# Rotary halves exchanged by lane shuffles on VectorE, with signed sine tables, where a constant matrix product did it

## What is computed

```python
def apply_rope(x, ang):
    cos = jnp.cos(ang)[None, :, None, :].astype(x.dtype)
    sin = jnp.sin(ang)[None, :, None, :].astype(x.dtype)
    x1, x2 = jnp.split(x, 2, axis=-1)
    return jnp.concatenate([x1 * cos - x2 * sin, x1 * sin + x2 * cos], axis=-1)

# in first_block:
qa_rope = apply_rope(qa_rope, ang_1d)                       # 8 heads, the last 32 of 96 features
k_pe = apply_rope(k_pe[:, :, None, :], ang_1d)              # one key, shared by the 8 heads
qb = jnp.concatenate([apply_rope(qr, ang_row), apply_rope(qc, ang_col)], axis=-1)   # 8 heads of 64
kb = jnp.concatenate([apply_rope(kr, ang_row), apply_rope(kc, ang_col)], axis=-1)   # 2 heads of 64
...
merged = jax.nn.sigmoid(gate_a) * ya + jax.nn.sigmoid(gate_b) * yb
```

## Time and profile before

| | us |
|---|---|
| median of three runs | 2274.43 |
| lowest, highest run | 2272.1, 2279.98 |
| span of the profiled execution | 2278.4 |
| TensorE busy in it | 2195.7 |
| VectorE busy in it | 1152.1 |
| ScalarE busy in it | 817.9 |
| GpSimd busy in it | 25.3 |

### The profile page before, as it was taken

How to read it: one execution, slowest core, us unless ns; L and a number is a source line. 1 busy time by engine, 2 the same in 40 slices (tenths; PEclk the granted TensorE clock), 3 DMA queues, 4 the chain that set the end, 5 groups by cost and what they waited for, 6 DMA issues and landing times. The chain is left out here.

```text
span 2278.4 us, 26492 instructions
## 1 busy us (share of the span) xinstructions
PE 2195.7 (96%) x10904; PEld 1735.5 (76%) x10904; DVE 1152.1 (51%) x1705; ACT 817.9 (36%) x1169; POOL 25.3 (1%) x22
## 2 busy tenths in 40 slices
PE   8999999999999998999988999999899998999998
PEld 6776668888888886887976888887686576888886
DVE  5456666542442577678745444422733636444423
ACT  4313663331232364442433322212514734332212
POOL 0001000000000000000000000000000000000000
PEclk9999999999999998999899999999999999999999
DMA  4221012322222222234112222222232021222221
GB/s 175 76 74 38 1 38 77 108 92 103 93 93 93 92 66 87 93 121 101 48 56 74 93 93 93 93 93 93 80 119 98 2 93 56 96 90 96 99 99 66
DMA packets 43113, 190.77 MB, mean 84 GB/s; under 512 B 15520, under 2 KB 16224, under 8 KB 22384
## 3 DMA queue, kind: packets, MB, share of 16 engines
q1 hardware_dynamic: 40656, 184.84, 24.1%
q10 hardware_dynamic: 2336, 4.23, 0.6%
HBM read 185.32 MB, written 3.74 MB: 83 GB/s over the span
## 5 line engine op out<-in xcount | busy, mean ns | idle before, releaser
L240 DVE TENSOR_TENSOR weights_low<-weights_raw,weights_high 128x2048 fp32r<-128x2048 f32 (+1 forms) x164 | 372.6, 2272 | 574.5 <-ACT weights_high L213 574.5
L421 PE MATMUL psum<-split,weights_high 128*128 128x512 f32 (+1 forms) x1496 | 598.2, 400 | 13.6 <-DVE weights_low L240 5.6
L423 PE MATMUL psum<-split,weights_low 128*128 128x512 f32 (+1 forms) x1496 | 597.0, 399 | 0.0
L422 PE MATMUL psum<-split,weights_high 128*128 128x512 f32 (+1 forms) x1496 | 592.7, 396 | 0.0
L213 ACT CAST weights_high<-weights_raw 128x2048 fp32r<-128x2048 f32 (+1 forms) x164 | 309.7, 1888 | 577.3 <-PE psum L423 545.1
L421 PEld LDWEIGHTS psum<-split,weights_high 128*128 128x128 f32 (+1 forms) x1496 | 282.3, 189 | 83.6 <-issue 11.6
L422 PEld LDWEIGHTS psum<-split,weights_high 128*128 128x128 f32 (+1 forms) x1496 | 282.5, 189 | 71.5 <-issue 1.7
L423 PEld LDWEIGHTS psum<-split,weights_low 128*128 128x128 f32 (+1 forms) x1496 | 282.3, 189 | 67.1
L423 PE MATMUL psum<-hidden_high,weights_low 128*128 128x512 f32 x256 | 102.1, 399 | 0.0
L422 PE MATMUL psum<-hidden_low,weights_high 128*128 128x512 f32 x256 | 100.9, 394 | 0.0
L421 PE MATMUL psum<-hidden_high,weights_high 128*128 128x512 f32 x256 | 100.4, 392 | 0.0
(11 more groups left out here) (463 smaller groups left out, 3069.4 us busy)
## 6 DMA issues: line engine op xcount, KB each, us to landing
weights_raw<-in_weights SPq DMA_DIRECT2D x161, 1024.0 KB, 4.8
minus_c<-minus_c_rows ACTq DMA_DIRECT2D x16, 256.0 KB, 8.4
x_stream<-in_x SPq DMA_DIRECT2D x4, 512.0 KB, 7.1
gdn_in_grown<-gdn_rows SPq DMA_DIRECT2D x4, 512.0 KB, 4.7
chain_grown<-gdn_rows SPq DMA_DIRECT2D x4, 512.0 KB, 4.0
out<-end_results SPq DMA_DIRECT2D x8, 256.0 KB, 2.0
table<-rope_tables SPq DMA_DIRECT2D x1, 1024.0 KB, 12.5
weights_raw<-in_weights SPq DMA_DIRECT2D x1, 768.0 KB, 4.3
```

The source lines that it names most:

```text
L240: self.nc.vector.tensor_tensor(out=self.low[:, n % 2, 0:width], in0=self.raw[:, n % 2, 0:width], in1=self.high[:, n % 2, 0:width].bitcast( ...
L421: nc.tensor.matmul(bank, wh, ah, start=first, stop=False)
L422: nc.tensor.matmul(bank, wh, al, start=False, stop=False)
L423: return nc.tensor.matmul(bank, wl, ah, start=False, stop=last)
```

## The change

The constant matrix `rotate` is dropped, and with it `rotate_tile` and its waits on TensorE. On VectorE each rotation first shuffles the partitions of its tile within each group of 32 (`stream_shuffle` with the list `other_half`, lane l takes lane l + 16 modulo 32) from the tile into `turned`. The minus sign that the matrix carried moves into the sine tables, which are negative for the first half of each group. The order then is: wait until the tile is normed (for `qk_b`), shuffle, wait for it, tile times cosine in place, `turned` times sine in place, wait for both, sum. All inputs of the two products now lie in SBUF. The loop's assignment of rotations to gates stays.

```diff
--- before.py
+++ after.py
@@ -50,7 +50,7 @@
 
 CONST_AT = {}
 _col = 0
-for _name, _n in [("identity", P), ("rotate", P), ("heads_of_pair", 2), ("ones", 1), ("causal_bias", P),
+for _name, _n in [("identity", P), ("heads_of_pair", 2), ("ones", 1), ("causal_bias", P),
                   ("earlier", P), ("before", P), ("not_after", P), ("eye", SOLVE * SOLVE)]:
     CONST_AT[_name] = (_col, _n)
     _col += _n
@@ -69,9 +69,6 @@
     row, col = np.arange(P)[:, None], np.arange(P)[None, :]
     put("identity", row == col)
 
-    half = ROPE // 2
-    first = (col % ROPE) < half
-    put("rotate", np.where(first & (row == col + half), -1.0, 0.0) + np.where(~first & (row == col - half), 1.0, 0.0))
     put("heads_of_pair", (row // HD_B) == np.arange(2)[None, :])
     put("ones", 1.0)
 
@@ -94,13 +91,13 @@
     for half in range(2):
         at = NOPE + half * (ROPE // 2)
         out[0, at:at + ROPE // 2] = np.cos(ang)
-        out[1, at:at + ROPE // 2] = np.sin(ang)
+        out[1, at:at + ROPE // 2] = np.sin(ang) if half else -np.sin(ang)
     row_ang = ((t // GRID_W).astype(np.float32)[None, :] * inv[:, None]).astype(np.float32)
     col_ang = ((t % GRID_W).astype(np.float32)[None, :] * inv[:, None]).astype(np.float32)
     for group in range(P // 16):
         a = row_ang if (group // 2) % 2 == 0 else col_ang
         out[2, group * 16:(group + 1) * 16] = np.cos(a)
-        out[3, group * 16:(group + 1) * 16] = np.sin(a)
+        out[3, group * 16:(group + 1) * 16] = np.sin(a) if group % 2 else -np.sin(a)
     return out
 
 
@@ -408,7 +405,7 @@
             at, n = CONST_AT[name]
             return const[:, at:at + n]
 
-        identity, rotate, ones = constant("identity"), constant("rotate"), constant("ones")
+        identity, ones = constant("identity"), constant("ones")
 
         def gain(name, tile=0):
             at = GAIN_AT[name] + tile
@@ -478,7 +475,8 @@
                     "squared", "added", "summed", "mean", "root", "inverted", "spread", "scaled", "high", "low")]
                 head_squared, head_summed, head_mean, head_root, head_inverted, head_spread, normed = [s.sem("head_" + n) for n in (
                     "squared", "summed", "mean", "root", "inverted", "spread", "normed")]
-                rotated, rotation_read, scaled, in_place = [s.sem(n) for n in ("rotated", "rotation_read", "scaled", "in_place")]
+                swapped, scaled, turned_scaled, in_place = [s.sem(n) for n in ("swapped", "scaled", "turned_scaled", "in_place")]
+                other_half = [(lane + ROPE // 2) % ROPE for lane in range(ROPE)]
 
                 def k_done(i):
                     return weights.tiles_before[latent_chunk + 1] + 3 * (i // 2) + i % 2 + 1
@@ -555,14 +553,6 @@
                                                             head_stat[:, 2, at + half:at + half + 1].broadcast_to([P, HD_B]),
                                                             identity, start=True, stop=True)
                             last.then_inc(head_spread, 1)
-
-                        def rotate_tile(n):
-                            tile, rows, _, _ = jobs[n]
-                            if n >= 2:
-                                pe.wait_ge(rotation_read, n - 1)
-                            if n >= n_a:
-                                pe.wait_ge(normed, n - n_a + 1)
-                            nc.tensor.matmul(psum[0:rows, 4 + n % 2, :], rotate[0:rows, 0:rows], tile, start=True, stop=True).then_inc(rotated, 1)
 
                         chunk_ready(c0)
                         high, low = weights.parts(Chunk(c0), DT)
@@ -625,10 +615,6 @@
                             if g % 2 == 0:
                                 chunk_ready(gate_chunk + g // 2)
                             whole_tile(gate_chunk + g // 2, g % 2, free(first_gate + g), split)
-                            if g == 1:
-                                pe.wait_ge(k_read, HEADS)
-                            for n in rotations.get(g, ()):
-                                rotate_tile(n)
                             if g in spreads:
                                 spread_heads(spreads[g])
 
@@ -710,14 +696,16 @@
                             buffer = turned[0:rows, n % 2, :]
                             if n >= 2:
                                 dve.wait_ge(in_place, n - 1)
-                            dve.wait_ge(rotated, n + 1)
-                            nc.vector.scalar_tensor_tensor(out=buffer, in0=psum[0:rows, 4 + n % 2, :], scalar=scale,
-                                                           in1=table[0:rows, at + 1, :], op0=ALU.mult,
-                                                           op1=ALU.mult).then_inc(rotation_read, 1)
+                            if n >= n_a:
+                                dve.wait_ge(normed, n - n_a + 1)
+                            nc.vector.stream_shuffle(buffer, tile, other_half).then_inc(swapped, 1)
+                            dve.wait_ge(swapped, n + 1)
                             nc.vector.scalar_tensor_tensor(out=tile, in0=tile, scalar=scale, in1=table[0:rows, at, :],
                                                            op0=ALU.mult, op1=ALU.mult).then_inc(scaled, 1)
-                            dve.wait_ge(rotation_read, n + 1)
+                            nc.vector.scalar_tensor_tensor(out=buffer, in0=buffer, scalar=scale, in1=table[0:rows, at + 1, :],
+                                                           op0=ALU.mult, op1=ALU.mult).then_inc(turned_scaled, 1)
                             dve.wait_ge(scaled, n + 1)
+                            dve.wait_ge(turned_scaled, n + 1)
                             nc.vector.tensor_tensor(out=tile, in0=tile, in1=buffer, op=ALU.add).then_inc(in_place, 1)
 
                         low(c0)
```

## The result

The changed kernel takes 2262.54 us (median of 4 runs, 2261.25 to 2265.61) beside 2277.14 for the kernel before, measured next to it: a ratio of 0.9939, 95% interval 0.9925 to 0.9954. Measured twice more on other occasions it gave 0.9938 (0.9925 to 0.995) and 0.9949 (0.9937 to 0.9962). The forecast was 2260.9, in a range of 2255 to 2268.

A forecast was written before the change was run, and what follows sets the result against it. The prediction took TensorE's issue order to bound the gate stage: removing fifteen rotation products gives 7.7 + 5.8 = 13.5 us, VectorE's added work stays hidden, so 2274.43 - 13.5 = 2260.9 us, range 2255 to 2268.

The forecast's parts named there:

- What bounds the stage: Gates 0 to 15: TensorE's issue order alone, busy 104.10 of 104.83 us; any product removed shortens it if VectorE keeps up.
- The sum of 13.5 us: Fifteen rotation products off TensorE: nine at gates 1 and 8 to 13 give 7.7 us, six at gates 2 to 7 give 5.8.
- rival 1: Gates 2 to 7: spreadings inherit the removed products' entrance, freeing nothing there; gain 7.7 us, time 2266.7; chance 0.08.
- The shuffle's duration: Each rotation on VectorE: one shuffle taken as 0.69 us, bounded above by 1.21 us, a scan on 512 columns.
- The self-wait: VectorE's rotation chain: 0.61 us between starts without a wait, 0.78 with one; the skill's rule would save 5.1 us of work.
- VectorE's lateness: Gates 10 to 13: VectorE falls some 2 to 2.5 us late by gate 13, covered by four banks and the last gates.
- Room to spare: VectorE over the whole gate stage: 73.7 us of work in 91.3 us, 17.6 us to spare.
- X: Duration of the shuffle in each rotation on VectorE; taken as 0.69 us.
- What comes behind: Stages behind the front: untouched, move forward as a block; first score to end about 2065.4 us.
- 2: VectorE becomes the bound mildly, with X between 1.9 and 3.2 us; at 2.5 us the time is 2270.5; chance 0.04.
- 3: VectorE makes the kernel slower, decided at X = 2.76 us; at 3.5 us the time is 2285.5; chance 0.03.
- 4: Behind the front, TensorE's stretches at the lower clock grow by 13 us, giving the gain back; time 2274; chance 0.05.

The follow-up runs named there:

- e1: Kernel before without its 15 rotation products on TensorE, VectorE's operations unchanged; ratio to before 0.9954, gate 0 to first score 99.51 us.
- e2: Changed kernel with 15 products of the same shape put back on TensorE, read by nobody; ratio to before 1.0007, gate 0 to first score 112.45 us.
- e3: Changed kernel with every shuffle done twice, each with its self-wait; median 2268.09 us, ratio to before 0.997.
- e4: Changed kernel with every shuffle done three times, each with its self-wait; median 2275.13 us, ratio to before 1.0001.
- e6: Changed kernel with every shuffle done four times, each with its self-wait; median 2284.55 us, ratio to before 1.0036.
- e9: Changed kernel with four more shuffles on VectorE behind the last eviction, holding back only the barrier; median 2268.80 us, ratio to before 0.9967.

## Why the prediction was right, point by point

The forecast was 2260.9 us, the median 2262.54. The mechanism held, and of the 1.6 us between them 0.6 is a mis-sized term (13.5 for 12.9). That the two are so near is in part luck: the forecast starts from a median of three runs that lie 8 us apart, 2274.43, which happens to be only 0.9 us under the 2275.3 of 50 runs.

- **What bounds the stage**: right. e1 and e2 move the first score by the products alone, to 0.03 us.
- **The sum of 13.5 us**: 12.91 in the gates. The nine products outside the spreadings gave 9 x 0.86, as said. The mis-sized term is that of gates 2 to 7, where I took the 0.96 us between the starts of product and spreading. They gave 7.68 - 6.82 = 0.86 each. Of the difference of 0.10 us, 0.08 is the entrance that rival 1 spoke of: the spreading now starts 0.31 us behind the split product, where the rotation product started 0.23 behind it. The row of the transposes at 0.23 us, on which I took 0.96, was the wrong neighbour: the load of their weights starts at 88.35 us, with the split product before them, and the spreading's starts only at 123.59, with the spreading itself, after 0.36 us in which nothing is loaded. Why it isn't loaded earlier stays open. Rival 1 was right in kind and wrong in size, 0.1 of 0.96 for each.
- **The shuffle's duration**: taken as 0.69 us, measured 0.73 to 0.76. The lower bound was misread: not every operation on 512 fp32 columns takes 0.69 us in the kernel before, as its 64 scalings of `attn_prob` (128x512, L932) take 484 ns each. Nothing came of it, as the shuffle is longer than either. Each call is two instructions; the first, LOAD_MASK_SELECT, takes 0.015 us or less and starts together with the shuffle. The Trainium skill's figure ("VectorE: DVE Perf Modes", section "The perf-mode tier table") had given an estimate of 0.80; this case's trace, with a median of 0.74, lies between it and 0.69. The loading of the permutation that the Trainium skill describes ("Vector Engine (DVE) Microarchitecture Reference", section 3.8) is there in the trace, and no cost of its own is seen.
- **The self-wait**: the chain of rows above has 0.61 us between starts without a wait and 0.78 with one, as before. The Trainium skill's rule ("VectorE: DVE Perf Modes", section "The DRAIN you can't avoid"), by which a semaphore between chained operations costs nothing extra, isn't borne out here: it costs 0.17 us.
- **VectorE's lateness**: forecast up to 2.5 us. The last eviction, for which VectorE waits, is at 196.99 us; two gates of 5.60 ahead of it TensorE had gate 13 ready, at 185.8. Its eviction starts at 188.35, 2.55 us late. Only the last gate makes it up, not the last two, as gate 13's own rotation and low half come behind its eviction; 2.36 us are left idle ahead of the last eviction:

```profile
188.35 0.69 DVE L781 TENSOR_TENSOR gates<-psum,factor 128x512 f32<-128x512 f32 x1
...
193.95 0.68 DVE L781 TENSOR_TENSOR gates<-psum,factor 128x512 f32<-128x512 f32 x1
196.99 0.69 DVE L781 TENSOR_TENSOR gates<-psum,factor 128x512 f32<-128x512 f32 x1 [2.36 <-PE psum L420]
```

- **Room to spare**: the step that failed, beside the term of 0.96. I counted 17.6 us as one pool, used up at X = 1.86 us. Idle time in gates 1 to 9 can't be kept for the six rotations of gates 10 to 13; what counts is the 2.36 us behind them. At X = 1.5 (e3) the first score is already 2.7 us late; the gain is gone at X = 2.3 (e4, 1.0001) where I had said 2.76; at X = 3.1 (e6) the kernel is slower, 1.0036. Part of that is the clock behind the barrier, of which the prediction's sum for long shuffles had nothing: by the first score alone e4 is still 112.42 - 108.10 = 4.3 us ahead of before, and the two would meet at about X = 2.6 (an estimate between e4 and e6). The result didn't hang on it, because X was 0.74.
- **What comes behind**: right that the later stages move forward as a block. Their length varies by several us from one execution to the next with the granted clock. By its own check, "about 2065.4 us", the prediction would count as wrong at 2060.21; the check was a poor one, as the same stages take 2057.4 to 2065.4 us in the profiles of these two kernels.
- **The rivals**: 2 and 3 didn't arise, but their mechanism is real and was reached by lengthening the shuffle. 4 (the gain given back by the clock) didn't arise on average: the mean clocks are alike, 0.983.

## What to carry to other kernels

A product taken from the queue of a saturated TensorE is worth the distance it puts between its neighbours, and the work that replaces it on another engine is free only while that engine's idle time lies behind it within the reach of the buffers: count the spare time from the densest group to the end of the stage, not over the whole stage. Price what remains by a row in which it already stands behind the same neighbour, since a small fp32 group may pay an entrance that the removed product paid for it. And compare executions at equal granted clock before a difference of a few us outside the edit is put down to the edit.

## What the runs showed of the hardware that I had not expected

- Beside GpSimd's copies (8.26 us, 167.04 to 175.30) VectorE's 512-column operations with two SBUF inputs took 0.81 to 1.09 us for their usual 0.69, and the shuffle, which has one, its usual 0.74 to 0.75. The low half of the weights, which also has two, took its usual 2.28 us where it began 0.23 us ahead of the copies; in before it began 0.03 us behind their start and took 2.72, and the copies 7.49 us. From the changed kernel's timelines, the copies and three operations within them:

```profile
167.04 8.26 POOL L683 COPY k_a<-k_pe 32x512 f32<-32x512 f32 x8 [166.60 <-DVE k_pe L709]
...
173.18 0.74 DVE L701 STREAM_SHUFFLE turned<-qk_b 128x512 f32<-128x512 f32 x1
173.95 0.87 DVE L703 SCALAR_TENSOR_TENSOR qk_b<-qk_b,table 128x512 f32<-128x512 f32 x1
174.75 1.09 DVE L705 SCALAR_TENSOR_TENSOR turned<-turned,table 128x512 f32<-128x512 f32 x1
```

- The distance from gate 0 to the first score repeats to 0.01 us over three profiles (99.51, 99.50, 99.50) and over e1, while whole executions of one kernel differ by 8 us. Stage distances settled here what medians couldn't.
- A TensorE that waited 4.8 us or more at the barrier came back at 0.50 of its clock in all four profiles that had such a stretch. After 2.3 us the clock fell in two of seven profiles, 0.6 to 0.8 us behind the first score. A fall cost 1.7 to 3.2 us over the next 22 us of the program, 2.1 in the one kernel (e9) that changes only the wait. What decides it in a given execution stays open.
